# An identity product written ahead of TensorE's waits in the second block of a two-block transformer kernel

## The chip, the cores and the metric

The kernel runs on one core of a Trainium2 chip. A core has TensorE (PE: matrix products; its weight loads are listed apart as PEld), VectorE (DVE), ScalarE (ACT), GpSimd (POOL) and SyncE (SP, which here only starts DMAs). Each engine runs its own instruction stream in order, and the streams meet at semaphores. The metric is the device time of one execution in microseconds (us), the median of several runs.

## The reference, cut to what matters

The input is one sequence of 512 tokens of width 1024, with 256 tokens of context and 256 of memory; all is float32. The first block (adaLN modulation, an RWKV, a neighbourhood attention and a convolution side by side, then a mixture of 16384 tiny experts whose rows are gathered by index) ends in `rmsnorm(xl, final_g)`. The second block, in which the change lies, then has two layers:

```
for layer in range(DEPTH_2):
    x = x + mixers[layer](rms_norm(x, mix_norms[layer]))
    xn, mn, wq, wkv, wo = xattn[layer]
    x = x + memory_cross_attention(rms_norm(x, xn), rms_norm(mem, mn), wq, wkv, wo)
    fn, wg, wu, wd = ffns[layer]
    x = x + swiglu(rms_norm(x, fn), wg, wu, wd)
return rms_norm(x, final_norm)
```

`mixers[0]` is a sliding-window attention beside a multi-head latent attention, `mixers[1]` a mixture of dilated windows; both have rotary positions. Attention is causal, so the second half of the tokens needs the keys of the first, but not the other way round.

## The kernel before

All of it is written by hand: for each engine there is one Python function a stage (`..._pe`, `..._act`, `..._dve`), which issues that engine's instructions in the order in which they are to run, with waits on semaphores. `wait_ge(signal, key)` waits until another engine has done a step; `claim(("bank", b), ...)` waits until a PSUM bank (there are eight) has been read by its last user. Activations lie transposed, the 1024 features over 8 chunks of 128 partitions, and tokens in the free dimension.

The second block is done in two halves of 256 tokens, h=0 and h=1. **Half 0** (1947 to 3156 us of the trace) is woven into the first block's expert stage: `peer_steps` hands the streams of both to each engine, and the second block's share advances in step with a cost that each function yields (`yield 4 * MM`, MM = 427 ns; PE, ACT and DVE must yield the same costs). Meanwhile POOL gathers the rows of the experts for tokens 256 to 511 and DVE multiplies and adds them; in that stretch PE has no expert work. **Half 1** (3156 us to the end) has the core to itself.

The stages of a half, on PE, are those of `second_pe`:

- `experts_pe`: 16 transposes that bring the experts' sums into the transposed layout.
- `scale_pe`, eight times a half: the RMS norm ahead of a stage. PE multiplies the squares by a matrix of ones (L2726, four products of 256 columns), ACT takes the root, DVE the reciprocal and then scales the eight chunks (L2751), and only then can the next products (L2681, in `product_pe`) start. Before it, PE waits until the last residual has been added (DVE), squared (ACT, L2700) and summed.
- `inputs_pe`, `latent_pe`, `dilated_pe`, `cross_pe`: the projections. `rotate_pe` (L3072) multiplies by a rotation matrix for the rotary positions, after ACT has copied the projection out of PSUM (L3065).
- `units_pe`: the attention, in units of one head and 128 queries. `unit_order` sets a pipeline: scores of unit u+1 (L2943), perhaps a store of a finished pair (transpose L2963, copied by ACT L3001 or DVE L3058), a piece of the next projection as filling (`fill.take`), the transposes of unit u's weights (L2950) after ACT's exponential, and the output of unit u-1 (L2957, 64 columns a product; 128 in the cross attention). The latent and dilated projections are the filling of the even and the dilated units; it runs out some units before the end, and the cross attention (8 units, twice a half) has none.
- `out_pe` and `ffn_pe`: long rows of products (L2681, L3447) that wait only for weights from HBM.

PSUM bank 0 holds sums of the first block and is not used by the second; `k.ident` is the 128x128 identity in SBUF.

Of the kernel before, what the change touches and what calls it, by code (L numbers as in the profile page):

```python
# [15 lines left out]
P = 128  # L16
# [2451 lines left out]
MM = 427  # L2468
# [183 lines left out]
    return x.rearrange("p (a b) -> p a b", b=TH)  # L2652


def load_wide(k, p, key, pieces, over=None):

    d = p.next_wide()
    for u in (2 * d, 2 * d + 1):
        p.claim(("w", u), k.S.proj_filled, over or key)
    for j, (dst, src) in enumerate(pieces(k.wide[d])):  # L2660
        p.e.dma_start(dst, src).then_inc(*p.up(k.S.landed(f"wide{d}"), (key, j)))
# [56 lines left out]
def scale_pe(k, p, a, tag, source):  # L2718

    S = k.S  # L2720
    p.wait_ge(S.residual_summed, (source, 2))
    p.wait_ge(S.residual_squared, (source, 3))
    p.claim(("bank", 3), S.norm_root, tag)
    parts = (a.sum[:, 0:TH], a.sum[:, TH:T], a.sq[:, 0:TH], a.sq[:, TH:T])
    for j, x in enumerate(parts):
        ins = p.e.matmul(k.bank[3][:, 0:TH], k.ones, x, start=j == 0, stop=j == 3, skip_group_check=True)  # L2726
    ins.then_inc(*p.up(S.norm_filled, tag))
    yield 4 * MM
    yield 2000
    yield 2000  # L2730
# [71 lines left out]
def experts_pe(k, p, a, tag):  # L2802
    S, e, h = k.S, k.peer, a.h_id
    for t in (2 * h, 2 * h + 1):
        for added in tile_combined(k, t):
            p.wait_ge(*added)
    for i in range(4):
        p.claim(("bank", 4 + i), S.residual_added, (tag, i))
        for c in (2 * i, 2 * i + 1):
            for t in range(2):  # L2810
                ins = p.e.transpose(k.bank[4 + i][:, c % 2 * TH + t * P:c % 2 * TH + t * P + P],
                                    e.ACC[2 * h + t][:, c * P:c * P + P], k.ident)
        ins.then_inc(*p.up(S.proj_filled, (tag, i)))
        yield 800


# [103 lines left out]


def units_pe(k, p, a, name, units, fill, rate):
    S = k.S
    for step, u in unit_order(units):
        x, key = units[u], (name, u)
        if step == "fill":
            yield from fill.take(rate, min(u + 1, len(units) - 1))
        elif step == "rest":
            yield from fill.rest()
        elif step == "pause":  # L2930
            yield unit_cost(x)
        elif step == "scores":
            yield from fill.until(x.mark, u - 1)
            for ready in x.ready:
                p.wait_ge(*ready)
            b = 2 + u % 2
            if x.nb < x.m:
                p.claim(("bank", b), S.weights_exp, key)
            else:
                p.claim(("bank", b), S.scores_low if x.sink is None else S.scores_biased, key)  # L2940
            c0 = 0
            for j, keys in enumerate(x.keys):
                ins = p.e.matmul(k.bank[b][:, c0:c0 + keys.shape[1]], x.q, keys, start=True, stop=True, skip_group_check=True)  # L2943
                c0 += keys.shape[1]
            ins.then_inc(*p.up(S.scores_filled, key))
        elif step == "weights":
            p.wait_ge(S.weights_exp, key)
            p.claim(("bank", 4), (S.act_weights, S.dve_weights)[u % 2], key)
            for j in range(x.m // P):
                ins = p.e.transpose(k.bank[4][:, j * P:j * P + P], a.S[u % 2][:, j * P:j * P + P], k.ident)  # L2950
            ins.then_inc(*p.up(S.weights_filled, key))
        elif step == "output":
            p.wait_ge((S.act_weights, S.dve_weights)[u % 2], key)
            p.wait_ge(*x.values_at)
            p.claim(("bank", 5), S.output_scaled, key)
            for j, values in enumerate(x.values):
                ins = p.e.matmul(k.bank[5][:, 0:x.w], a.PT[u % 2][:, j * P:j * P + P], values, start=j == 0,  # L2957
                                 stop=j == len(x.values) - 1, skip_group_check=True)
            ins.then_inc(*p.up(S.output_filled, key))
        elif step == "store":  # L2960
            p.wait_ge(S.output_scaled, key)
            p.claim(("bank", 4), (S.act_stored, S.dve_stored)[x.tile % 2], key)
            p.e.transpose(k.bank[4][:, 0:P], a.O[x.tile], k.ident).then_inc(*p.up(S.store_filled, key))  # L2963
# [104 lines left out]

def rotate_pe(k, p, a, j, out, rot, key, rows=P):
    n = out.shape[1]  # L3070
    p.wait_ge(k.S.raw_ready, key)
    p.e.matmul(out, rot[0:rows, 0:rows], a.raw[0:rows, j, 0:n], start=True, stop=True, skip_group_check=True).then_inc(  # L3072
        *p.up(k.S.rotation_filled, key))
# [146 lines left out]
def latent_pe(k, p, a):  # L3220

    S, h = k.S, a.h_id
    n = TH * (h + 1)
# [10 lines left out]
    uq = [landed_wide(k, p, ("uq", h, j))[:, 0:1152].rearrange("p (c n) -> p c n", n=384) for j in range(2)]  # L3234
    ukv = landed_wide(k, p, ("ukv", h)).rearrange("p (c n) -> p c n", n=D)
    heads = ukv.rearrange("p c (h n) -> p c h n", n=P)
    p.wait_ge(S.normed, (("latent", h), 4))
    for t in range(2 * h + 2):
        p.claim(("bank", 6), S.act_emptied, ("latent_v", h, t))
# [622 lines left out]
```

## Time and profile before

| | us |
|---|---|
| median of 3 runs | 4306.85 |
| the three runs | 4305.0 to 4326.61 |
| profiled execution | 4309.87 |
| its span, first to last instruction | 4308.0 |

The page of the profile gives PE 3514.9 us busy (82% of the span), PEld 2569.9 (60%), DVE 2216.5 (51%), POOL 1369.1 (32%) and ACT 710.7 (16%). The mean clock that was granted to TensorE is 0.875 of full speed; it has two levels, 1.2 and 2.4 GHz (0.50 and 1.00 in the views). A row of the timeline is a merged run of like instructions: start, length, engine, line, operation, tiles, shape, count, and in brackets how long the engine sat idle before it and what ended that. An ordinary float32 product of the kernel is two MATMUL records in the trace, a transpose is one.

### The profile page before, as it was taken

How to read it: one execution, taken by the hardware profiler on the slowest of the kernel's cores; microseconds unless marked ns; L12 is line 12 of the kernel's file. 1: busy time of each engine (PE TensorE's matmuls, PEld its weight loads, DVE VectorE, ACT ScalarE, POOL GpSimd, SP SyncE). 2: the span in 40 equal slices, each digit the busy share in tenths (PEclk: the TensorE clock that was granted, in tenths of full speed). 3: DMA queues.
4: the chain of work that ended last, by engine and by line, in shares of the span. 5: the costliest groups of instructions: out<-in, count | busy, mean ns of one | idle time of the engine just before them, and what ended most of it. 6: DMA issues, size and time to landing. Idle time of an engine off the chain costs nothing. (4 is left out here: it accounts for less than half of the span.)

```text
span 4308.0 us, 39665 instructions
## 1 busy us (share of the span) xinstructions
PE 3514.9 (82%) x14550; PEld 2569.9 (60%) x14550; DVE 2216.5 (51%) x4375; ACT 710.7 (16%) x1582; POOL 1369.1 (32%) x1215
## 2 busy tenths in 40 slices
PE   7888987887667777756778988779877889999898
PEld 3446657786323343424456776667754678777687
DVE  2443144445887878867677568776543310132201
ACT  2112122221211111111211001210012110021100
POOL 0550012211566666764245555455400000000000
PEclk9887898998888898987688999889977889997999
DMA  6320300004899899997479999889920134321343
GB/s 194 88 86 10 91 25 1 1 22 139 301 328 339 320 356 329 379 336 290 142 254 333 387 368 320 278 281 391 348 81 30 49 104 151 129 86 40 98 150 105
DMA packets 452343, 835.61 MB, mean 194 GB/s; under 512 B 46707, under 2 KB 294574, under 8 KB 452142
## 3 DMA queue, kind: packets, MB, share of 16 engines
q0 software_dynamic: 147456, 536.94, 34.0%
q1 hardware_dynamic: 304694, 296.13, 21.7%
q8 instruction: 117, 1.92, 0.2%
q14 instruction: 76, 0.62, 0.0%
HBM read 830.80 MB, written 2.17 MB: 193 GB/s over the span
## 5 line engine op out<-in xcount | busy, mean ns | idle before, releaser
L2681 PE MATMUL banks<-arena 128*128 128x256 f32 (+1 forms) x4992 | 1167.5, 394 | 92.7 <-DVE arena L2751 44.6
L2681 PEld LDWEIGHTS banks<-arena 128*128 128x128 f32 (+1 forms) x4992 | 983.1, 199 | 270.5 <-issue 67.1
L2246 POOL DMA_INDIRECT arena<-in_peer_u,arena x512 | 571.8, 1117 | 577.2 <-DVE arena L2375 221.7
L2246 POOL DMA_INDIRECT arena<-in_peer_v,arena x512 | 576.6, 1126 | 445.3 <-DVE arena L2361 282.7
L2375 DVE CUSTOM_DVE_ANT_0 arena<-arena 128x1024 f32<-128x1024 f32 x512 | 628.1, 1227 | 101.0 <-DMA arena<-in_peer_u,arena 84.4
L2319 PE MATMUL banks<-arena 128*128 128x512 f32 x768 | 416.5, 686 | 237.7 <-ACT arena L2337 157.6
L2319 PEld LDWEIGHTS banks<-arena 128*128 128x128 f32 x768 | 156.2, 217 | 463.6 <-issue 262.1
L2361 DVE SCALAR_TENSOR_TENSOR arena<-arena 128x1024 f32<-128x1024 f32 x316 | 406.2, 1286 | 29.6 <-DMA arena<-in_peer_v,arena 19.4
L3447 PE MATMUL banks<-arena 128*128 128x256 f32 x1408 | 310.5, 378 | 0.0
L3489 DVE TENSOR_TENSOR arena<-banks,arena 128x512 f32<-128x512 f32 x44 | 30.5, 692 | 538.2 <-PE banks L2681 538.2
L3447 PEld LDWEIGHTS banks<-arena 128*128 128x128 f32 x1408 | 266.2, 189 | 37.8
L835 PE MATMUL banks<-arena 128*128 128x512 f32 (+1 forms) x320 | 136.1, 574 | 28.4 <-ACT arena L962 11.6
L2943 PE MATMUL banks<-arena 64*128 64x256 f32 (+6 forms) x384 | 145.6, 490 | 3.8 <-issue 2.6
L3468 ACT ACTIVATE arena<-banks 128x512 f32<-128x512 f32 x44 | 26.3, 598 | 703.8 <-PE banks L2681 703.7
L548 PE MATMUL banks<-arena 128*128 128x512 f32 (+1 forms) x384 | 140.9, 527 | 0.0
L2950 PE MATMUL banks<-arena 128*128 128x128 f32 x360 | 87.9, 345 | 64.6 <-ACT arena L3001 35.2
L2957 PE MATMUL banks<-arena 128*128 128x64 f32 (+1 forms) x720 | 136.3, 333 | 2.2 <-DVE arena L3052 2.2
L2957 PEld LDWEIGHTS banks<-arena 128*128 128x128 f32 x720 | 132.5, 262 | 6.0 <-issue 5.0
L2986 ACT ACTIVATE arena<-arena 128x256 f32<-128x256 f32 (+3 forms) x128 | 69.4, 542 | 388.8 <-DVE arena L3025 287.9
L2950 PEld LDWEIGHTS banks<-arena 128*128 128x128 f32 x360 | 52.5, 172 | 119.4 <-issue 61.0
L2063 PE MATMUL banks<-arena 128*128 128x512 f32 (+1 forms) x320 | 118.6, 522 | 3.5 <-ACT arena L1841 3.5
L510 POOL TENSOR_TENSOR arena<-arena 128x2048 f32<-128x2048 f32 x16 | 57.3, 3601 | 198.0 <-ACTq L278 105.7
(328 smaller groups left out, 4108.6 us busy)
## 6 DMA issues: line engine op xcount, KB each, us to landing
arena<-in_l_w_gate SPq DMA_DIRECT2D x44, 1024.0 KB, 6.8
arena<-in_l_w_up SPq DMA_DIRECT2D x44, 1024.0 KB, 9.2
arena<-in_l_w_down SPq DMA_DIRECT2D x44, 1024.0 KB, 5.6
arena<-in_ada_w SPq DMA_DIRECT2D x24, 1024.0 KB, 8.1
arena<-in_l_w_qkv SPq DMA_DIRECT2D x24, 1024.0 KB, 8.4
arena<-in_w_in SPq DMA_DIRECT2D x36, 512.0 KB, 4.0
arena<-in_l_w_out SPq DMA_DIRECT2D x16, 1024.0 KB, 5.2
arena<-in_peer_q_w SPq DMA_DIRECT2D x20, 512.0 KB, 7.0
```

The costliest lines, as they stand in the source:

```text
L548: ins = p.e.matmul(k.bank[b][0:m, 0:n], k.W[slot][:, c, 0:m], rhs(c), start=c == 0, stop=c == c_n - 1, skip_group_check=True)
L835: ins = p.e.matmul(k.bank[b][0:m, 0:n], k.W[slot][:, c, 0:m], rhs(c), start=c == 0, stop=c == c_n - 1, skip_group_check=True)
L2063: ins = p.e.matmul(k.bank[4][:, cols], ws[j][:, c, :], k.HT[:, c, cols], start=c == 0, stop=c == DC - 1, skip_group_check=True)
L2246: p.e.indirect_dma_start(e.ring[slot], None, tables[table], bass.IndirectOffsetOnAxis(ap=e.IDX[h][:, t, j:j + 1], axis=0)).then_inc(*p.up( ...
L2319: ins = p.e.matmul(k.bank[b], e.diag[x % 4], e.ring[slot][:, half * T:half * T + T], start=h == 0 and j == 0, stop=h == HEADS - 1 and j == ...
L2361: p.e.scalar_tensor_tensor(out=e.ACC[t], in0=e.ring[slot], scalar=factor, in1=e.ACC[t], op0=ALU.mult, op1=ALU.add).then_inc(*p.up(S.rows_a ...
L2375: p.e.tensor_tensor_reduce(out=e.prod, in0=e.ring[slot], in1=e.H2[:, t, :], scale=1.0, scalar=0.0, op0=ALU.mult, op1=ALU.add, accum_out=e. ...
L2681: ins = p.e.matmul(out, left(c), right(c), start=c == 0, stop=c == c_n - 1, skip_group_check=True)
L2943: ins = p.e.matmul(k.bank[b][:, c0:c0 + keys.shape[1]], x.q, keys, start=True, stop=True, skip_group_check=True)
L2950: ins = p.e.transpose(k.bank[4][:, j * P:j * P + P], a.S[u % 2][:, j * P:j * P + P], k.ident)
L2957: ins = p.e.matmul(k.bank[5][:, 0:x.w], a.PT[u % 2][:, j * P:j * P + P], values, start=j == 0, stop=j == len(x.values) - 1, skip_group_che ...
L3447: ins = p.e.matmul(k.bank[4 + o // 2][:, o % 2 * TH:o % 2 * TH + TH], w[:, r, P * o:P * o + P], a.hid[:, (i - 1) % 2, TH * r:TH * r + TH], ...
```

## The change

A new function `occupied(k, p, n)` issues n products of the identity with itself into the first 128 columns of bank 0. Nothing reads that bank afterwards, and no wait, signal or yielded cost is added. It is called

- 8 times over (n=8) ahead of the first wait of `scale_pe`, and 8 more right behind its four products, that is, ahead of the wait for the scaled chunks;
- with n=2 behind each of the four groups of transposes in `experts_pe`, with n=2 ahead of the wait in `rotate_pe`, and with n=8 ahead of the wait of `latent_pe` for its normed inputs;
- with n=1 in `units_pe` ahead of the waits of `weights` and of `output`, in units whose filling came to less than 4 * MM.

```diff
+def occupied(k, p, n):
+
+    for _ in range(n):
+        p.e.matmul(k.bank[0][:, 0:P], k.ident, k.ident, start=True, stop=True, skip_group_check=True)
...
 def scale_pe(k, p, a, tag, source):
 
     S = k.S
+    occupied(k, p, 8)
     p.wait_ge(S.residual_summed, (source, 2))
     p.wait_ge(S.residual_squared, (source, 3))
     p.claim(("bank", 3), S.norm_root, tag)
...
     ins.then_inc(*p.up(S.norm_filled, tag))
+    occupied(k, p, 8)
     yield 4 * MM
...
         ins.then_inc(*p.up(S.proj_filled, (tag, i)))
+        occupied(k, p, 2)
         yield 800
...
         if step == "fill":
-            yield from fill.take(rate, min(u + 1, len(units) - 1))
+            filled = 0
+            for n in fill.take(rate, min(u + 1, len(units) - 1)):
+                filled += n
+                yield n
...
         elif step == "weights":
+            if filled < 4 * MM:
+                occupied(k, p, 1)
             p.wait_ge(S.weights_exp, key)
...
         elif step == "output":
+            if filled < 4 * MM:
+                occupied(k, p, 1)
             p.wait_ge((S.act_weights, S.dve_weights)[u % 2], key)
...
 def rotate_pe(k, p, a, j, out, rot, key, rows=P):
     n = out.shape[1]
+    occupied(k, p, 2)
     p.wait_ge(k.S.raw_ready, key)
...
     heads = ukv.rearrange("p c (h n) -> p c h n", n=P)
+    occupied(k, p, 8)
     p.wait_ge(S.normed, (("latent", h), 4))
```

It comes to 544 identity products, 282 in half 0 and 262 in half 1. In half 1 they are 8 in `experts_pe`, 128 in `scale_pe`, 32 in `rotate_pe`, 8 in `latent_pe` and 86 in `units_pe` (31 in the even units, 23 in the dilated ones, 32 in the two cross attentions). In half 0 the even units have 51. On the other engines nothing changes.

On PE, the dilated units of half 1 where the filling ends. The rows of before: transposes (L2950), outputs (L2957), scores (L2943), a store (L2963):

```order
L2681 MATMUL banks<-arena 128x256 x8
L2950 MATMUL banks<-arena 128x128 x3
L2957 MATMUL banks<-arena 128x64 x4
L2943 MATMUL banks<-arena 128x256 x2
L2963 MATMUL banks<-arena 128x128
L2950 MATMUL banks<-arena 128x128 x3
L2957 MATMUL banks<-arena 128x64 x3
L2943 MATMUL banks<-arena 128x256 x2
L2950 MATMUL banks<-arena 128x128 x4
```

The same place in the changed kernel, where L2964, L2973, L2955 and L2979 are those four lines and L2658 is the identity product:

```order
L2687 MATMUL banks<-arena 128x256 x8
L2964 MATMUL banks<-arena 128x128 x3
L2973 MATMUL banks<-arena 128x64 x4
L2955 MATMUL banks<-arena 128x256 x2
L2979 MATMUL banks<-arena 128x128
L2658 MATMUL banks<-arena 128x128
L2964 MATMUL banks<-arena 128x128 x3
L2658 MATMUL banks<-arena 128x128
L2973 MATMUL banks<-arena 128x64 x3
L2955 MATMUL banks<-arena 128x256 x2
L2658 MATMUL banks<-arena 128x128
L2964 MATMUL banks<-arena 128x128 x4
```

From the first unit without filling on, one product stands ahead of the transposes and one ahead of the outputs of each unit.

On PE, the end of that stage: the output projection, the norm ahead of the second cross attention, and that attention's first unit, before:

```order
L2963 MATMUL banks<-arena 128x128
L2681 MATMUL banks<-arena 128x256 x64
L2726 MATMUL banks<-arena 128x256 x4
L2681 MATMUL banks<-arena 128x256 x32
L2943 MATMUL banks<-arena 128x256 x2
L2950 MATMUL banks<-arena 128x128 x2
```

and now:

```order
L2979 MATMUL banks<-arena 128x128
L2687 MATMUL banks<-arena 128x256 x64
L2658 MATMUL banks<-arena 128x128 x8
L2733 MATMUL banks<-arena 128x256 x4
L2658 MATMUL banks<-arena 128x128 x8
L2687 MATMUL banks<-arena 128x256 x32
L2955 MATMUL banks<-arena 128x256 x2
L2658 MATMUL banks<-arena 128x128
L2964 MATMUL banks<-arena 128x128 x2
```

Eight products fill the wait on each side of the norm's four.

## Rows read from the trace of the kernel before

**Rows 1.** The page: clock granted to TensorE in 40 slices, tenths of full speed.

```profile
PEclk9887898998888898987688999889977889997999
```

**Rows 2.** Busy time of each engine, granted clock and DMA by stretch.

```profile
core 0: us, PE busy (x) PEld busy (x) DVE busy (x) ACT busy (x) POOL busy (x), PEclk, DMA share, GB/s
...
2047.00:2191.00 144.00, 101.25 (x320) 65.69 (x320) 91.25 (x247) 31.55 (x107) 33.88 (x37) 0.62 0.50 153
...
2344.00:2563.00 219.00, 196.65 (x859) 168.38 (x860) 141.19 (x173) 13.92 (x19) 123.69 (x108) 0.95 1.03 389
...
2730.00:2763.00 33.00, 24.13 (x79) 16.87 (x79) 21.87 (x65) 7.79 (x29) 8.43 (x9) 0.50 0.58 181
...
3244.00:3317.00 73.00, 50.30 (x178) 31.60 (x177) 28.64 (x99) 20.11 (x59) 0.00 (x0) 0.81 0.05 15
3317.00:3406.00 89.00, 75.86 (x282) 48.00 (x282) 31.57 (x104) 22.20 (x59) 0.00 (x0) 0.69 0.07 24
...
3907.50:3960.00 52.50, 45.98 (x164) 37.29 (x164) 15.42 (x51) 10.97 (x29) 0.00 (x0) 0.50 0.03 10
...
4017.00:4036.00 19.00, 11.79 (x67) 7.88 (x67) 8.75 (x29) 6.21 (x23) 0.00 (x0) 1.00 0.02 7
```

**Rows 3.** Timeline of PE, dense projection rows at full clock, half 1.

```profile
3212.47 3.73 PE L3127 MATMUL banks<-arena 128*128 128x128 f32 x32
```

**Rows 4.** Timeline of PE, first cross attention of half 1.

```profile
3459.26 0.44 PE L2950 MATMUL banks<-arena 128*128 128x128 f32 x2 [1.70 <-ACT arena L2990]
...
3464.14 1.06 PE L2957 MATMUL banks<-arena 128*128 128x128 f32 x4
...
3484.79 0.48 PE L2963 MATMUL banks<-arena 128*128 128x128 f32 x1 [0.52 <-DVE arena L3052]
```

**Rows 5.** Timeline of PE, second cross attention of half 1.

```profile
4017.10 0.44 PE L2950 MATMUL banks<-arena 128*128 128x128 f32 x2 [1.70 <-ACT arena L2990]
...
4021.31 0.61 PE L2957 MATMUL banks<-arena 128*128 128x128 f32 x4
...
4036.38 0.33 PE L2963 MATMUL banks<-arena 128*128 128x128 f32 x1 [0.52 <-DVE arena L3052]
```

**Rows 6.** Timeline of PE, end of the dilated units, half 1.

```profile
3904.49 1.00 PE L2957 MATMUL banks<-arena 128*128 128x64 f32 x8
3905.43 1.13 PE L2943 MATMUL banks<-arena 64*128 64x256 f32 x4
...
3907.78 0.77 PE L2950 MATMUL banks<-arena 128*128 128x128 f32 x3 [0.97 <-DVE arena L3058]
...
3917.31 1.09 PE L2950 MATMUL banks<-arena 128*128 128x128 f32 x4 [1.39 <-ACT arena L3001]
3918.19 1.81 PE L2957 MATMUL banks<-arena 128*128 128x64 f32 x8
...
3923.94 2.07 PE L2943 MATMUL banks<-arena 64*128 64x256 f32 x4
...
3927.24 0.87 PE L2950 MATMUL banks<-arena 128*128 128x128 f32 x3 [0.82 <-DVE arena L3058]
...
3960.34 30.65 PE L2681 MATMUL banks<-arena 128*128 128x256 f32 x128
```

**Rows 7.** Chain that ended last within 3900 to 3965 us, by line.

```profile
by line: PE banks L2943 28.1%; PE banks L2957 27.5%; PE banks L2950 16.8%; PE banks L2681 12.8%; DVE arena L3025 5.0%; issue 2.9%; ACT arena L2986 2.2%; PE banks L2963 1.5%; DVE arena L3052 1.4%; DVE arena L3058 1.0%; ACT arena L3001 1.0%; 
```

**Rows 8.** Timeline of PE, norms of half 1 and what follows them.

```profile
3741.77 3.75 PE L2726 MATMUL banks<-arena 128*128 128x256 f32 x8 [4.11 <-ACT arena L2700]
3748.49 10.03 PE L2681 MATMUL banks<-arena 128*128 128x256 f32 x32 [2.96 <-DVE arena L2751]
...
3992.55 1.97 PE L2726 MATMUL banks<-arena 128*128 128x256 f32 x8 [1.56 <-issue]
3997.48 17.05 PE L2681 MATMUL banks<-arena 128*128 128x256 f32 x64 [2.96 <-DVE arena L2751]
...
4036.55 14.02 PE L2681 MATMUL banks<-arena 128*128 128x256 f32 x64
```

**Rows 9.** Timeline of PE, two rotations among the dilated units of half 1.

```profile
3804.07 1.10 PE L3072 MATMUL banks<-arena 128*128 128x512 f32 x2 [2.08 <-ACT arena L3065]
...
3846.86 2.04 PE L3072 MATMUL banks<-arena 128*128 128x512 f32 x2 [2.02 <-ACT arena L3065]
```

More of the change, by code:

```diff
@@ L2922, in units_pe @@
 def units_pe(k, p, a, name, units, fill, rate):
-    S = k.S
+    S, filled = k.S, 0
     for step, u in unit_order(units):
```

## The prediction

> **What bounds the kernel now.** I read the page first, for the clock row: in 11 of the last 22 slices, which are those of the second block, TensorE is granted less than 0.9 of full speed [rows 1]. Then the table of stretches, to see where that is. The long rows of products run at 0.95 and are bound by DMA in half 0 (DMA share 1.03). The attention stretches are the slow-clocked ones: 0.62, 0.50, 0.81, 0.69 and 0.50, while the second cross attention of half 1 stands at 1.00 [rows 2]. Third, the timeline of PE there. In the last 52.5 us of half 1's dilated units PE is busy for 45.98 us at clock 0.50 [rows 2], and the chain view of 3900 to 3965 us runs for over 85% over PE's own lines [rows 7]. So PE is the bound, and at half speed: eight output records that took 1.00 us just before take 1.81, four score records 2.07 instead of 1.13 [rows 6]. Nothing long was waited for when the clock went: the wait in front of the first slow transposes was 0.97 us, the longest later one 1.39 [rows 6]. In that stage products are short, and the clock stays low until the dense products at 3960.
>
> How the clock reacts is also seen in pairs of like places. The two cross attentions of half 1 are the same code: from its first transposes to its last store one takes 3484.79 - 3459.26 = 25.53 us at half speed, the other 4036.38 - 4017.10 = 19.28 us at full [rows 4, 5]. A norm behind a wait of 4.11 us takes 3.75 us for its ones products against 1.97 behind 1.56 us; 64 product records behind a norm take 17.05 us where 64 behind no wait take 14.02 [rows 8]. A rotation behind 2.08 us of waiting ran at full speed (1.10), another behind 2.02 us at half (2.04) [rows 9]. The waits are near a border where it can go either way.
>
> **The price of an added product.** 32 records of 128 columns take 3.73 us at full speed, so 0.117 each at most, and a product is two of them: 0.22 us (two such records at the pace without the last one's tail) [rows 3]. At half speed four such records take 1.06 instead of 0.61 us, so a product costs 0.43 to 0.45 us [rows 4, 5]. 544 of them are 120 us at full speed; what counts is how much does not fit into waits.
>
> **Where they fit.** Ahead of the norms: 8 products are 1.76 us. The wait behind a feed-forward is 4.11 us, behind an output projection 1.56 plus the last product's tail of about 0.16, so they cost 0 to 0.1 us. Behind the ones products: 1.76 us in a wait of 2.96 us [rows 8]; at half speed they are 3.5 us and would overshoot by some 0.4. At rotations 0.44 us lie in about 2.0 [rows 9]. In a unit, the product ahead of the transposes lies in a wait only where a store came before (0.97 and 1.39 us, two units in four [rows 6]); the one ahead of the outputs lies in none, since the copy of those weights was done a unit earlier. That one is on PE's path: 0.22 us a unit, and where there is no store 0.44.
>
> **What comes back if the clock holds, half 1.**
> - End of the dilated units. Four units take 3927.24 - 3907.78 = 19.46 us, of which 2.2 are waits, so 17.2 is PE at half speed [rows 6]; at full speed that is 8.9. The waits for DVE and ACT do not shrink, and with a faster PE they grow: I put 3.1 us in place of 2.2, for 12.0. The added products not covered by waits are 2 x 0.22 + 4 x 0.22 = 1.3. So 13.3 for 19.46; over the stretch of 52 us (2.7 times four units) 16.5 us come back. The 128 records behind it take 30.65 us, at 14.02 for 64 they would take 27.9 [rows 6, 8]: 2.8. Together 19.
> - Cross attentions: the first gains 25.53 - 19.28 = 6.25, and both pay 8 x 0.22 = 1.8: net 2.7.
> - Latent part. 3317 to 3406 us: clock 0.69 is 62% of 89 us at half, 55 us, of which PE is busy 0.85, 47 us; half of it is 23. Against it stand 31 products, two thirds uncovered, 4.5, and waits that grow, 3. Net 16. From 3244 to 3317 the filling is always 4 MM or more, so hardly a product is added and the alternating clock (0.81) stays; 1 us from one rotation.
> - Norms. The one at 3741 gives 1.8 for its own products and 10.03 - 7.0 = 3.0 for those behind it (32 records at 14.02 / 64 each); the one at 3992 gives 17.05 - 14.02 = 3.0 [rows 8]. There are eight of them a half: of the others two lie behind a wait of about 10 us which 1.8 us of products do not fill, and give 1 to 3 behind them; the last one and the transposes behind it give 3. Together 14.
> - Two rotations at half speed give 0.9 each and as much for the products behind: 3.
>
> Sum: 19 + 2.7 + 17 + 14 + 3 = 56 us.
>
> **Half 0.** The same stages: 33 us at 0.50 (end of the dilated units), 144 at 0.62 (latent) [rows 2], two cross attentions. By the same steps: 8, a third of the 38 us that 144 us would yield (109 us at half speed, PE 0.70 busy) = 12 because waits for DVE, which also sums expert rows, are longer and more of the clock falls remain, 3, norms 10, rotations 3, together 36. Not all of it reaches the end: in its product rows DMA is full (1.03), and DVE does expert rows between block steps [rows 2]. Bounds for what passes are nothing and all; I take a little over half, as the attention stretches themselves have DMA free (0.50, 0.58): 20.
>
> Forecast: 56 + 20 = 76 us less. The profiled execution would go from 4309.87 to about 4234, and the median, 3 us below that, from 4306.85 to **4231**.
>
> **Rivals.**
> - *Clock holds, half 0 passes nothing or all.* 4251 or, with all 36, 4215; with waits that do not grow, the latent and dilated terms at 23 and 25 and half 0 full, about 113 less: 4194. Same mechanism, another size.
> - *Only the long waits are mended.* The clock does not fall at norms and rotations (14 + 3 + 1, 10 + 3 in half 0), but units of short products still drop it, as they did behind 0.97 us of wait, and then pay 0.43 us a product. Gains about 25, costs as in the next rival 25: about 4305. The Trainium skill (TensorE: Matmul & The Clock Gate, section on what is actually happening) says that the ramp costs less than 1% of a typical kernel span; by that at most 43 us are to be had in all, 4264. The rows speak against both: half speed in the dilated end alone costs 19 us, and that end is not behind a long wait [rows 6].
> - *The identity product does not count for the clock, or too little (slower).* It is mostly zeros. Then all slow stretches stay slow and each product on PE's path costs 0.43. End of the dilated units: 8 x 0.43 = 3.4 per four units, 0.9 covered, 2.5, times 2.7 is 7; first cross 4 x 0.9 = 3.5, second 1.8; latent 31 x 0.43 x 0.7 = 9; eight norms at half speed 2; half 1: 23, half 0, where waits are longer, 11. 4341. It decides itself at the first unfilled units: if 3907 to 3960 is still at 0.50, this has won. For it speaks only that the trace has no such product; against it that every other kind of product raised the clock.
> - The same page, in its section on PE-mode transpose, says that transposes do not bring the full clock. The change uses a plain matrix product, so by that page it counts; the sum is the same.
>
> **How the numbers follow.** Forecast as worked out 0.60; same mechanism with more or less of it 0.18; only long waits 0.13; slower 0.09. A measurement of this kernel can tell about 0.5% (21.5 us) from no change. Faster by more: 0.60 + 0.18 + a little of the third = 0.80. Within 0.5%: 0.12. Slower: 0.08. The range leaves out the slower rival and the outer part of the third: 4194 to 4295.
>
> **What would show it.** In the profile after: the stretch of the last dilated units of half 1 at clock above 0.9 and about 36 us long; both cross attentions of half 1 near 21 us; ones products of norms behind feed-forwards 1.97 us; the mean clock above 0.93; the added line busy at 0.22 us a product. Wrong, if the clock in the units stays at 0.50, if half 0 (1947 to 3156) does not get shorter though its clock rises, or if the waits for ACT and DVE in the units grow by what PE saves.

## The result, and the profile after

The changed kernel takes 4260.29 us, the median of 4 runs (4257.88 to 4275.26), against 4307.60 for the kernel before beside it (4305.0 to 4326.61): ratio 0.9883, with a 95% interval of 0.9857 to 0.9909. A second measurement with more rounds gave 4257.57 against 4309.04, 0.9882 (0.9857 to 0.9907). The two medians are 47 and 51 us below the kernel before; the forecast was 76, so 4260 lies inside the range and 29 us above the number.

Where the time went is read by stretches. First the table of stretches for half 0 and half 1 as wholes, of the kernel before, then of the kernel after (the columns are those of [rows 2]: start:end, length, busy time of each engine with its instructions in brackets, granted clock, DMA share, GB/s):

```profile
1947.00:3155.50 1208.50, 980.82 (x4059) 791.94 (x4060) 848.69 (x1354) 176.93 (x399) 566.36 (x488) 0.85 0.83 300
3155.50:4308.00 1152.50, 1019.54 (x4451) 828.69 (x4450) 245.74 (x606) 158.97 (x363) 0.00 (x0) 0.89 0.30 95
```

```profile
1942.70:3161.80 1219.10, 1033.62 (x4622) 855.44 (x4623) 848.29 (x1354) 177.03 (x399) 571.56 (x489) 0.89 0.82 297
3161.80:4258.30 1096.50, 1009.50 (x4976) 839.78 (x4974) 245.74 (x606) 159.13 (x363) 0.00 (x0) 0.97 0.31 100
```

**Half 1 is 56.0 us shorter (1152.5 to 1096.5), half 0 is 10.6 us longer.** In half 1 the clock went from 0.89 to 0.97, and PE, with 525 more instructions, was busy for 10 us less and idle for 46 us less (133.0 to 87.0). In half 0 the clock went up as well, from 0.85 to 0.89; PE was idle for 42 us less (227.7 to 185.5), but busy for 53 us more. The other 4 us lie ahead of half 0, where nothing was changed; that part ends between 1940 and 1980 us from kernel to kernel in the traces of this study.

The page's clock row of after, to be set beside [rows 1]: its last 11 slices, half 1, read 8, 8 and then nine times 9; in half 0, the 11 slices ahead of them, values of 7 and 8 remain.

```profile
PEclk9888988999888898979788999799988999999999
```

By stages (each cut runs from one norm's ones products to the next norm's; the last to the end), half 1 of the kernel before: sliding-window and latent attention; first cross attention; feed-forward; dilated attention; second cross attention; feed-forward; last norm.

```profile
3182.10:3437.10 255.00, 214.20 (x842) 152.80 (x843) 78.41 (x235) 53.27 (x142) 0.00 (x0) 0.81 0.15 47
3437.10:3502.20 65.10, 51.47 (x209) 40.00 (x209) 19.99 (x47) 13.56 (x34) 0.00 (x0) 0.79 0.23 73
3502.20:3741.80 239.60, 232.52 (x1065) 202.09 (x1065) 17.41 (x26) 12.14 (x19) 0.00 (x0) 0.99 0.46 149
3741.80:3992.60 250.80, 227.46 (x1017) 184.81 (x1017) 72.46 (x191) 46.03 (x108) 0.00 (x0) 0.85 0.19 62
3992.60:4052.20 59.60, 45.84 (x209) 36.30 (x209) 20.01 (x47) 13.51 (x34) 0.00 (x0) 0.94 0.25 79
...
4291.70:4308.00 16.30, 9.18 (x24) 5.57 (x24) 7.02 (x11) 2.84 (x4) 0.00 (x0) 0.50 0.16 64
```

The same six of after:

```profile
3188.60:3424.90 236.30, 205.73 (x985) 154.46 (x986) 78.33 (x235) 53.43 (x142) 0.00 (x0) 0.92 0.16 51
3424.90:3483.10 58.20, 50.21 (x274) 41.22 (x273) 20.02 (x47) 13.43 (x34) 0.00 (x0) 1.00 0.26 81
3483.10:3721.40 238.30, 234.81 (x1098) 204.10 (x1098) 17.40 (x26) 12.15 (x19) 0.00 (x0) 1.00 0.46 150
3721.40:3947.20 225.80, 211.04 (x1126) 175.09 (x1127) 72.49 (x191) 46.07 (x108) 0.00 (x0) 0.99 0.21 69
3947.20:4005.50 58.30, 50.32 (x274) 41.33 (x274) 20.01 (x47) 13.54 (x34) 0.00 (x0) 1.00 0.26 81
...
4243.80:4258.30 14.50, 8.17 (x40) 6.09 (x40) 7.02 (x11) 2.83 (x4) 0.00 (x0) 0.79 0.18 72
```

Line by line: 18.7, 6.9, 1.3, 25.0, 1.3 and 1.8 us less, with 1.2 for the second feed-forward. The gain sits where the clock was low, and DVE and ACT are busy for as long as before in every stage.

Half 0, from its second norm to its third (sliding-window and latent attention), before and after:

```profile
1974.00:2222.40 248.40, 188.68 (x707) 138.45 (x707) 177.15 (x365) 48.06 (x141) 91.60 (x85) 0.73 0.66 223
```

```profile
1968.50:2227.90 259.40, 206.88 (x889) 161.67 (x890) 177.00 (x365) 48.15 (x141) 92.81 (x85) 0.81 0.64 215
```

This stage alone is 11.0 us longer, about as much as all of half 0: the clock rose from 0.73 to 0.81, the idle time fell by 7 us, and PE was busy for 18 us more. Part of the 11 may be chance: the other two traces with products in half 0 took 256.2 and 253.5 us for it, and the seven with the full experts' work and no products there 248.4 to 255.0.

The end of the dilated units of half 1, timeline of PE after (start, length, operation; in brackets the idle time ahead and who ended it). L2658 is the added product, L2964 the transposes, L2973 the outputs; the rows answer to [rows 6]:

```profile
3894.93 0.52 PE L2964 MATMUL banks<-arena 128*128 128x128 f32 x3 [0.74 <-DVE arena L3074]
...
3901.68 0.63 PE L2964 MATMUL banks<-arena 128*128 128x128 f32 x4 [1.30 <-ACT arena L3017]
3902.15 0.39 PE L2658 MATMUL banks<-arena 128*128 128x128 f32 x2
3902.37 1.00 PE L2973 MATMUL banks<-arena 128*128 128x64 f32 x8
...
3908.31 0.52 PE L2964 MATMUL banks<-arena 128*128 128x128 f32 x3 [0.74 <-DVE arena L3074]
...
3917.74 27.89 PE L2687 MATMUL banks<-arena 128*128 128x256 f32 x128
3945.46 1.95 PE L2658 MATMUL banks<-arena 128*128 128x128 f32 x16
3947.24 1.92 PE L2733 MATMUL banks<-arena 128*128 128x256 f32 x8
```

Four units take 3908.31 - 3894.93 = 13.38 us, where they took 19.46; eight output records are back at 1.00. The waits are about as long as before (0.74 and 1.30 us, with a product already inside them), yet the clock stays up. The added line costs (3947.24 - 3945.46) / 8 = 0.22 us a product.

Now the same place in half 0, the end of its dilated units, before and after:

```profile
2736.93 0.66 PE L2950 MATMUL banks<-arena 128*128 128x128 f32 x2 [1.62 <-ACT arena L3001]
...
2748.59 0.66 PE L2950 MATMUL banks<-arena 128*128 128x128 f32 x2 [1.68 <-ACT arena L3001]
```

```profile
2740.62 0.66 PE L2964 MATMUL banks<-arena 128*128 128x128 f32 x2 [1.37 <-ACT arena L3017]
2741.07 0.64 PE L2658 MATMUL banks<-arena 128*128 128x128 f32 x2
2741.50 0.95 PE L2973 MATMUL banks<-arena 128*128 128x64 f32 x4
...
2754.62 0.66 PE L2964 MATMUL banks<-arena 128*128 128x128 f32 x2 [1.42 <-ACT arena L3017]
```

Two transposes take 0.66 us in both: half speed in both. Four units went from 11.66 to 14.00 us. Here the products are paid for (2741.50 - 2741.07 = 0.43 us each) and buy nothing. The stretch of the table says it too:

```profile
2738.00:2771.00 33.00, 29.03 (x106) 22.74 (x106) 18.55 (x55) 5.85 (x23) 6.57 (x7) 0.50 0.44 127
```

### The profile page after: what moved, and what is told of

Read it like the earlier page. It is cut to its first block and busy times, and to the rows that moved or that the text cites. A ratio compares the mean times of both kernels' runs of the same rounds, so it can differ in the third digit from the quotient of the medians.

```text
span 4258.3 us, 41827 instructions
## 1 busy us (share of the span) xinstructions
PE 3555.5 (83%) x15638; PEld 2641.1 (62%) x15638; DVE 2219.7 (52%) x4375; ACT 711.5 (17%) x1582; POOL 1379.1 (32%) x1215
## 3 DMA queue, kind: packets, MB, share of 16 engines
q8 instruction: 125, 2.05, 0.2%
## 5 line engine op out<-in xcount | busy, mean ns | idle before, releaser
L2687 PE MATMUL banks<-arena 128*128 128x256 f32 (+1 forms) x4992 | 1142.1, 388 | 78.3 <-DMA arena<-in_l_w_up 35.4
L2687 PEld LDWEIGHTS banks<-arena 128*128 128x128 f32 (+1 forms) x4992 | 954.9, 194 | 254.3 <-issue 40.9
L2246 POOL DMA_INDIRECT arena<-in_peer_v,arena x512 | 588.8, 1150 | 446.0 <-DVE arena L2361 284.9
L2319 PEld LDWEIGHTS banks<-arena 128*128 128x128 f32 x768 | 156.6, 217 | 461.0 <-issue 265.7
L3465 PEld LDWEIGHTS banks<-arena 128*128 128x128 f32 x1408 | 265.6, 189 | 38.3
L2658 PE MATMUL banks<-arena 128*128 128x128 f32 x1088 | 189.0, 302 | 0.0
L2658 PEld LDWEIGHTS banks<-arena 128*128 128x128 f32 x1088 | 171.3, 217 | 22.2 <-issue 16.9
L2955 PE MATMUL banks<-arena 64*128 64x256 f32 (+6 forms) x384 | 124.8, 430 | 3.0 <-issue 2.3
L835 PEld LDWEIGHTS banks<-arena 128*128 128x128 f32 x320 | 63.3, 207 | 92.9 <-issue 81.4
L1566 POOL TENSOR_TENSOR arena<-arena 64x256 f32<-64x256 f32 x24 | 19.1, 796 | 313.4 <-ACT arena L1465 312.5
```

The lines of the kernel that those rows point to most:

```text
L835: ins = p.e.matmul(k.bank[b][0:m, 0:n], k.W[slot][:, c, 0:m], rhs(c), start=c == 0, stop=c == c_n - 1, skip_group_check=True)
L2246: p.e.indirect_dma_start(e.ring[slot], None, tables[table], bass.IndirectOffsetOnAxis(ap=e.IDX[h][:, t, j:j + 1], axis=0)).then_inc(*p.up( ...
L2319: ins = p.e.matmul(k.bank[b], e.diag[x % 4], e.ring[slot][:, half * T:half * T + T], start=h == 0 and j == 0, stop=h == HEADS - 1 and j == ...
L2658: p.e.matmul(k.bank[0][:, 0:P], k.ident, k.ident, start=True, stop=True, skip_group_check=True)
L2687: ins = p.e.matmul(out, left(c), right(c), start=c == 0, stop=c == c_n - 1, skip_group_check=True)
L3465: ins = p.e.matmul(k.bank[4 + o // 2][:, o % 2 * TH:o % 2 * TH + TH], w[:, r, P * o:P * o + P], a.hid[:, (i - 1) % 2, TH * r:TH * r + TH], ...
```

## The experiments

Theory A: the products keep TensorE's clock up, half 1 gives the whole gain, and half 0 passes little of it on, because DVE's expert rows set its pace. Rival B: half 0 gets 20 us shorter, as the forecast had it. (The expectations of the first two runs also name a "Theory B", which is another thing: the products of half 0 neither cost nor gain.) Rival C: what counts is any instruction in PE's stream that keeps it issuing, not the load. Each kernel ran beside the kernel before on the same chip; the ratio is to that one. The first four share one chip, the next three another, the last four a third; the kernel before took 4321.9, 4318.52 and 4307.51 us there.

**One half alone.** Of the 544 products, 262 are in half 1 and 282 in half 0.

```diff
-def occupied(k, p, n):
+def occupied(k, p, a, where, n):
-    for _ in range(n):
+    for _ in range(n if a.h_id == 1 else 0):
```

> The change in half 1 only (262 products). Theory A: the gain is made in half 1 alone, where TensorE is on the path, and the products of half 0 cost 6 to 11 us: about 4308 - 56 = 4252, and half 1 takes 1096 us. Theory B: the products of half 0 neither cost nor gain, the 11 us there are chance of where the clock falls: 4260. If half 0 gave something hidden: above 4265.

Measured: 4285.23 us (4275.8 to 4295.31) against 4321.9, ratio 0.9911 (0.9877 to 0.9945). Its four times form two pairs, 4275.8 and 4277.18, 4293.28 and 4295.31. In the median that is 37 us less, not 56: by its own expectation the result lies on the side of "half 0 gave something hidden", although the faster pair is 45 us less and the intervals of this kernel and of the change overlap. The profiled one is of the upper pair, its half 1 took 1122.2 us, and its timeline shows what the 17 us are:

```profile
3898.87 0.33 PE L2979 MATMUL banks<-arena 128*128 128x128 f32 x1
3899.04 0.39 PE L2658 MATMUL banks<-arena 128*128 128x128 f32 x2
3900.73 0.78 PE L2964 MATMUL banks<-arena 128*128 128x128 f32 x4 [1.31 <-ACT arena L3017]
3901.31 0.63 PE L2658 MATMUL banks<-arena 128*128 128x128 f32 x2
...
3911.74 0.88 PE L2964 MATMUL banks<-arena 128*128 128x128 f32 x3 [0.39 <-DVE arena L3074]
...
3934.07 0.88 PE L2964 MATMUL banks<-arena 128*128 128x128 f32 x3 [0.39 <-DVE arena L3074]
```

At 3899 a product takes 0.39 us in the display, behind the wait of 1.31 it takes 0.63: the clock fell there, although the same instructions with the same 1.30 us of wait held it in the profile of the change. From then on four units take 3934.07 - 3911.74 = 22.3 us, 2.9 more than without the products. So the products make the fall less likely; they do not exclude it: the dilated stage took 250.8, 250.8, 250.8, 250.8 and 246.8 us in the five traces without products in its units, and 224.8 to 225.8 us in five of the eight traces that have them, or the transposes in their place, at full size, 249.5 (this one), 244.9 and 243.3 in the other three. Where the clock falls, the same code costs instead of saving, until the next dense row.

The opposite half:

```diff
-    for _ in range(n):
+    for _ in range(n if a.h_id == 0 else 0):
```

> The change in half 0 only (282 products). Theory A: 4308 + 6 to 11 = 4314 to 4319, since the clock that comes back there meets waits for DVE, ACT and DMA, and the products in units at half speed lie on the path. Theory B: 4308, within noise. My prediction had it at 4288.

Measured: 4328.19 (4313.1 to 4347.5) against 4321.9, ratio 1.0009 (0.9985 to 1.0033): from 6 us less to 14 us more. Rival B's 20 us less are outside; the 6 to 11 us more of Theory A and the nothing of "Theory B" both lie inside. Its table of stretches for half 0:

```profile
1961.50:3181.80 1220.30, 1032.65 (x4623) 855.32 (x4624) 848.51 (x1354) 176.60 (x399) 564.24 (x489) 0.90 0.82 297
```

Clock 0.90 instead of 0.85, length 1220.3. Half 0 measures 1205.6 to 1217.1 us in the seven traces where it has no products (before, the single-half and other half-1 kernels), and 1214.0, 1219.1 and 1220.3 in the three where it has them: no gain, and a loss of some 7 us of which part may be chance. (On the chip of this run the three without took 1211.1 to 1217.1.)

**Is it the load or the instruction?** Two kernels with products in half 1 only. In one, each is replaced by two transposes of the identity, instruction for instruction at the same places; in the other the same product reads 32 of the 128 rows.

```diff
-        p.e.matmul(k.bank[0][:, 0:P], k.ident, k.ident, start=True, stop=True, skip_group_check=True)
+        for _ in range(2):
+            p.e.transpose(k.bank[0][:, 0:P], k.ident, k.ident)
```

> Half 1 only, and each product is replaced by two transposes of the identity (one trace record each, as a product has two, so the same time). By what the Trainium skill states (TensorE: Matmul & The Clock Gate, PE-mode transpose) transposes do not bring the full clock: 4320 to 4335. If they count as products do, as the 16 transposes ahead of 3157 us in the trace of before suggest, where the clock went up behind them: 4252.

Measured: 4284.49 (4276.06 to 4289.59) against 4321.9, ratio 0.9919 (0.9892 to 0.9946). Half 1:

```profile
3180.00:4274.20 1094.20, 1005.80 (x4975) 831.98 (x4973) 245.71 (x606) 159.00 (x363) 0.00 (x0) 0.98 0.32 101
```

Transposes do what the products do: clock 0.98, half 1 in 1094.2 us, and the ratio is that of the run half1 (0.9911). The Trainium skill (TensorE: Matmul & The Clock Gate, section on PE-mode transpose) says that transposes do not bring the full clock. For the transpose instruction as this kernel issues it, float32 against the identity, this trace differs, and the measurement decides.

```diff
-        p.e.matmul(k.bank[0][:, 0:P], k.ident, k.ident, start=True, stop=True, skip_group_check=True)
+        p.e.matmul(k.bank[0][:, 0:P], k.ident[0:32, :], k.ident[0:32, 0:P], start=True, stop=True, skip_group_check=True)
```

> Half 1 only, and each product contracts over 32 partitions of the identity in place of 128: the same 128 columns and the same time on TensorE, a quarter of the array's rows. If the gain is the granted clock, and the clock follows how much of the array works: the clock stays as before and the products cost their time, 4320 to 4335. If any product counts alike: 4252, as with full rows. If the gain were not the clock but something in the order or spacing of the instructions: 4252 too.

Measured: 4390.08 (4386 to 4416) against 4321.9, ratio 1.0157 (1.0131 to 1.0184). Half 1 by the table, and the end of its dilated units:

```profile
3196.70:4414.40 1217.70, 1152.20 (x4976) 917.79 (x4974) 245.92 (x606) 159.94 (x364) 0.00 (x0) 0.87 0.28 90
```

```profile
3998.84 0.79 PE L2658 MATMUL banks<-arena 32*128 32x128 f32 x2
3999.57 1.97 PE L2973 MATMUL banks<-arena 128*128 128x64 f32 x8
```

As many columns in as many instructions, PE busy for 95% of half 1 (92% in the change), and yet the clock of half 1 is 0.87, below the 0.89 without them: rival C falls, since an instruction that keeps PE issuing is not enough, and so does the thought that the order of the instructions makes the gain. The cost was underestimated (4320 to 4335 expected): at half speed such a product takes 3999.57 - 3998.84 = 0.73 us, where a full one takes 0.43. The weight loads in the traces show part of why. The load of a full product begins 0.21 us ahead of the product (3901.10 against 3901.31 in the run half1); that of the small one begins with it at 3998.84, and PEld sat idle for 0.33 us before. Eight small ones in a row are hardly dearer (2.05 us at full speed, 1.95 for full ones). So this kernel differs from the change in two things, in the load and in these gaps, and no run here tells which of them keeps the clock down.

**Which products.** Half 1 only, those of the attention units alone (86), then those of the norms alone (128).

```diff
-    for _ in range(n if a.h_id == 1 else 0):
+    for _ in range(n if a.h_id == 1 and where == "unit" else 0):
```

> Half 1, and only the 86 products in the attention units (none at norms, rotations, the latent start). My prediction's terms (dilated end 19, cross 2.7, latent 16): up to 38 us less, 15 to 20 less in those executions in which the clock falls at the entry of the dilated end. If the long waits at norms and rotations are what counts, and the units only pay: 0 to 10 us more.

Measured: 4286.95 (4275.58 to 4303.01) against 4318.52, ratio 0.9915 (0.9892 to 0.9939). As good as all 262 within the intervals. Its times spread over 27 us, and in the profiled one the dilated stage took 243.3 us, not 225.8: this execution lost the clock there. Its first stage is 16 us shorter than before (255.1 to 238.7), as much as the forecast's latent term.

The second kernel has `where == "norm"` in that line.

> Half 1, and only the 128 products at the eight norms. My prediction's term: 14 us less, seen at the norms behind feed-forwards (3.75 to 1.97 us for the ones products) and in the 32 to 64 products behind each norm; the units stay as before. If the clock behind a norm carries over into the units: the first cross attention at full speed as well, 20 less. If 8 products overshoot the short waits: 5 less or nothing.

Measured: 4314.56 (4308.27 to 4349.16) against 4318.52, ratio 0.9998 (0.9971 to 1.0026). In its trace half 1 is 3.6 us shorter than before (1148.9). The two feed-forwards and the dilated stage gain 6.5 us, and the second cross attention's stage loses 5.4, because there the clock fell in this execution:

```profile
3991.10:4056.10 65.00, 54.77 (x242) 43.85 (x241) 19.99 (x47) 13.48 (x34) 0.00 (x0) 0.79 0.23 72
```

The norms' products alone are worth nothing that can be measured. That what they mend is given back in the next attention is how this one trace has it; whether the other executions lost it in the same place is not known.

**Only where PE waits.** Products in half 1 only; none ahead of outputs; ahead of transposes only behind a store, there 4 (cross) or 6 (other units) where ACT copies the store, and 2 or 4 where DVE does; seven ahead of each latent value after the first, 32 in place of 8 at the latent start; 28 in place of 8 ahead of the half's first norm and the last. The lines that differ from the change, less those of the norms and the latent start:

```diff
-            if filled < 4 * MM:
-                occupied(k, p, 1)
+            if filled < 4 * MM and stored is not None:
+                occupied(k, p, a, "unit", (4 if x.w == P else 6) if stored % 2 == 0 else (2 if x.w == P else 4))
+            stored = None
             p.wait_ge(S.weights_exp, key)
...
-            if filled < 4 * MM:
-                occupied(k, p, 1)
...
+        if t:
+            occupied(k, p, a, "latent", 7)
         p.claim(("bank", 6), S.act_emptied, ("latent_v", h, t))
```

> Half 1 only, with the products put where PE waits: in the units none ahead of outputs and none where no store came before, but 6 or 4 ahead of the transposes behind a store (4 or 2 in the cross attention); 7 ahead of each latent value product that waits for ACT, 32 for the latent start, 28 ahead of the two norms behind waits of 10 us. If the products ahead of outputs lie on the path, 0.22 us each, and the alternating clock of 3244 to 3317 costs some 7 us: 15 to 20 us less than the same half with the products as in the change (half 1 about 1080 us), and no dilated end at half speed. If the products ahead of outputs cost nothing because the waits behind them shrink as much: within 8 us of it.

Measured: 4255.35 (4250.2 to 4263.28) against 4318.52, ratio 0.985 (0.9806 to 0.9894), half 1 in 1086.0 us, 10.5 less than in the change. The end of the dilated units:

```profile
3875.53 0.52 PE L2965 MATMUL banks<-arena 128*128 128x128 f32 x3
...
3886.35 1.06 PE L2658 MATMUL banks<-arena 128*128 128x128 f32 x8
3887.48 0.52 PE L2965 MATMUL banks<-arena 128*128 128x128 f32 x3
```

Four products in a row, with no wait left behind them, and four units in 3887.48 - 3875.53 = 11.95 us instead of 13.38. The second cross attention takes 19.29 us from its first transposes to its last store, as it did before the change at full clock (19.28, [rows 5]), where the change takes 20.37. So the products outside waits cost what they were priced at, and the clock is held without them. The expectation of 15 to 20 us was too high all the same, since the dilated stage as a whole gained only 1.0 us. Of the 10.5 us, 5.6 are in the first stage (latent), 1.9 at the first norm, the rest in the cross and dilated stages and at the last norm; the parts were not tried one by one. This is the fastest version, though its interval and that of the change overlap, and the two did not run on one chip.

**What sets the pace of half 0.** Two pairs, each with and without the change. In the first pair the expert rows of tokens 256 to 511 are gathered at half their width, from other places of the tables, while DVE works on 1024 columns as before; in the second DVE too works on 512. Neither computes the experts' sums for these tokens as it should. The first pair says what DMA holds back. The second lightens DMA and DVE together, so it says what DVE holds back once DMA is light; DVE's work alone was not halved in any run.

```diff
-        p.e.indirect_dma_start(e.ring[slot], None, tables[table], bass.IndirectOffsetOnAxis(
+        place, rows = e.ring[slot], tables[table]
+        if t >= 2:
+            place, rows = place[:, 0:T], rows.rearrange("n (a b) -> (n a) b", b=T)
+        p.e.indirect_dma_start(place, None, rows, bass.IndirectOffsetOnAxis(
...
```

> The kernel before, with the gathered expert rows of tokens 256 to 511 half as wide (2 KB in place of 4, from other places of the tables), DVE's work on them unchanged; that part of the result is wrong by it. It is the base for the next one. If half 0 is bound by DMA in its feed-forwards and not elsewhere: half 0 gets shorter by the waits for weights, 45 us, and not by more.

> The same with the change in both halves. If DMA takes back what the clock gives in half 0: against the last one 56 us less in half 1 and 20 to 36 less in half 0. If it is DVE's expert rows between block steps, or the clock itself does not hold there: 56 less in all, half 0 within 10 us of equal.

Measured: 4249.23 without and 4210.6 with the change (ratios 0.9852 and 0.977 to the kernel before): 39 us for the change. Half 0 of the two traces:

```profile
1955.90:3097.10 1141.20, 957.59 (x4058) 779.51 (x4059) 848.56 (x1354) 177.16 (x399) 548.80 (x491) 0.87 0.63 205
```

```profile
1951.60:3095.80 1144.20, 1010.37 (x4622) 844.62 (x4623) 848.34 (x1354) 176.79 (x399) 546.52 (x490) 0.91 0.63 204
```

Half 0 without the change got 67 us shorter by the narrow rows (1208.5 to 1141.2; 45 were expected), so DMA does hold it back. But with DMA share down from 0.83 to 0.63 the change still gives nothing in half 0, so DMA is not what takes the change's gain. Half 1 gave 37.6 us in this pair and not 56 (1153.0 to 1115.4), because the profiled execution lost the clock in the dilated stage (244.9 us).

```diff
...
+                x = slice(0, T if t >= 2 else D)
-                p.e.tensor_tensor_reduce(out=e.prod, in0=e.ring[slot], in1=e.H2[:, t, :], scale=1.0, scalar=0.0, op0=ALU.mult,
+                p.e.tensor_tensor_reduce(out=e.prod[:, x], in0=e.ring[slot][:, x], in1=e.H2[:, t, x], scale=1.0, scalar=0.0, op0=ALU.mult,
...
```

> As narrow_before, and DVE's multiply and add over those rows half as wide too (1024 to 512 columns); half of that part of the expert sums is left out. Base for the next. Waits of PE for DVE's block work in half 0 should shrink by 0.6 us each, some 50 to 100 us in all.

> The same with the change. If DVE's expert rows are what half 0 waits for: 56 less in half 1 and 20 to 36 less in half 0 against light_before. If the clock in half 0 does not hold because there are too few products for its longer waits, then with shorter waits it holds: the same gain. If neither: half 0 equal, 56 less in all.

Measured: 4197.16 without and 4132.45 with the change (0.9743 and 0.9601): 65 us. Half 0 of the two traces:

```profile
1946.80:3050.10 1103.30, 955.39 (x4059) 777.63 (x4060) 586.12 (x1354) 177.14 (x399) 521.37 (x491) 0.87 0.65 211
```

```profile
1939.70:3025.10 1085.40, 979.79 (x4623) 821.83 (x4624) 585.63 (x1354) 177.25 (x399) 520.19 (x491) 0.94 0.66 215
```

With DVE busy for 586 us instead of 849, the change makes half 0 17.9 us shorter, and its clock reaches 0.94. What differs between the pairs is PE's busy time. The idle time falls by 42 us in the original pair, by 50 in the narrow and by 42 in the light one; the busy time grows by 53, 53 and 24. Had DVE's full rows taken back what a faster PE saves, the idle time would have fallen by less in the first two pairs than in the light one, and it did not; PE's waits for DVE fell in the original pair too (80.7 to 70.7 us in all). The light rows let more of the clock come back: both pairs stand at 0.87 without the change, and at 0.91 and 0.94 with it. That is the second branch of the expectation above, in which shorter waits let the clock hold. It rests on one trace each, and the light one with the change is the fastest of its kernel's four times (4122.58, median 4132.45). Yet the end of its dilated units stays slow even here:

```profile
2655.00:2676.00 21.00, 19.50 (x71) 15.26 (x70) 9.78 (x36) 4.17 (x15) 4.72 (x5) 0.50 0.22 64
```

and the whole dilated stage takes 209.8 us with the products and 209.9 without. The gain is in the first stage (237.5 to 232.7 us, clock 0.75 to 0.87) and in the first cross attention (69.1 to 62.9 us, clock 0.78 to 1.00; in the original pair it stayed at 0.79, and 71.8 became 73.5).

## Why the prediction was right or wrong, point by point

**What bounds the kernel, and that the products hold the clock: right.** The slower rival had put its test at the first unfilled units of half 1. They ran at 1.00, not 0.50; the identity's zeros did not keep it from counting. The rival of long waits alone falls with the same rows. The prediction took a bound of 43 us for it from the Trainium skill (TensorE: Matmul & The Clock Gate, section on what is actually happening: the ramp costs under 1% of a typical kernel span). That bound was misread: the section gives the figure for the ramp at the start of a kernel, and here the clock fell and rose all through the second block. Half 1 alone gave back 56 us, 1.3% of the span and 5% of its own length. No run here measures the ramp at the start.

**Half 1: right in its sum and in most terms.** Forecast 56, measured 56.0. That it agrees to the last digit is luck: two other traces with the same products give 1095.8 and 1095.6 us for half 1, two more 1115.4 and 1122.2, which is 30 to 57 us less than the 1152.5 of before.
- The dilated end: four units forecast at 13.3, measured 13.38; the stretch of 52.56 us [rows 6: 3907.78 to 3960.34] took 36.2 (forecast 36); the 128 records behind it 27.89 (forecast 27.9).
- Cross attentions: forecast near 21 each, both 20.37. The cost of the eight units' products was put at 1.8 and is 20.37 - 19.28 = 1.1, since those ahead of transposes fit into waits more often than assumed.
- Latent: forecast 17 with one rotation; its stage, which also holds the products behind a norm, is 18.7 shorter.
- Norms: forecast 14. The rows that were looked at agree (ones products 3.75 to 1.97 behind the feed-forward at 3721, 1.8 at the last norm). As a whole the term was not measured: latent, norms and rotations together gave 56 - 19.2 (dilated end) - 4.1 (cross attentions) = 32.7, forecast 34. Taken alone the norms' products gave 3.6 us in the trace and no measurable time (norms1), so most of the term needs the units' products beside it. The terms of this sum are not independent, which the working did not say.
- Products outside waits: priced at 1.3 us per four units. The kernel with none there is 13.38 - 11.95 = 1.43 faster: right.
- Two sums of the rivals do not come out of their own terms: the "about 113" behind the range's lower end adds up to some 105 (4202, not 4194), and "costs as in the next rival 25" stands beside 23 + 11 = 34 there. Neither touches the forecast.

**Half 0: wrong, and this is the whole miss.** The failed step is "By the same steps: 8, a third of the 38 us ... = 12 ..., together 36", of which 20 were to pass. Measured: 10.6 us more in the profiles of the change, 1.0009 (0.9985 to 1.0033) for half 0 alone. The prediction blamed what might not reach the end; what failed comes before that, the 36 us themselves. PE was to be busy for less, and was busy for 53 us more, while its idle time fell by 42.
- *The dilated end (8).* The step carried half 1's reaction over to units that are not the same. In half 0 a unit has fewer records (1 or 2 transposes for 3 or 4, 2 or 4 outputs for 6 or 8) beside waits for ACT that are not shorter (1.62 and 1.68 us, 1.39 in half 1). One product ahead of each wait did not raise the clock (0.50 in the change, 0.50 with light experts), and four units took 14.00 - 11.66 = 2.3 us more. The wait rows for this were in the trace and were not set against half 1's.
- *Latent, cross attentions, norms, rotations (28).* Here the clock did rise, but too little: in the first stage from 0.73 to 0.81 (half 1's went from 0.81 to 0.92), in the first cross attention not at all in the profile of the change (0.79; 0.88 in that of half0). At a low clock an added product costs 0.43 us and not 0.22, and the products outside waits cost more than the clock gave back: the first stage took 248.4 to 259.4 us.
- *What passes (20 of 36).* The fraction was taken from the free DMA of those stretches. DMA did not take the gain (narrow pair: 3 us more). With DVE's expert rows halved as well the change gains 18 us in half 0, and the rows show it as a higher clock, not as waits that stop growing. "DVE does expert rows between block steps" was in the text, and what it does to the clock was not priced. That DVE's rows act through the length of PE's waits fits these rows and was not tested by itself.

The prediction named its own refutation, half 0 not shorter though its clock rises; that is what happened. Its mark of a mean clock above 0.93 was missed as well, at 0.91, since half 0 stayed at 0.89.

**The steadiness of the gain** was not considered. Whether a stretch keeps its clock differs between executions of the same kernel when it is near the border (half1: 17 us between its pairs of times). All ten timed runs of the change lie between 4250.8 and 4275.3, so this hit it little; the profiled execution of narrow_after lost 19 us in its dilated stage by it.

**Left open.** How much of the loss in half 0, some 7 us and 10.6 in the profiles, is the price of products outside waits and how much is chance. Also why half 1 with products alone gained 37 us in the median (45 in its faster pair) where the full change gained 47 to 51: half 0's products may make the state in which half 1 begins better, or the chips differ; nothing here tells these apart. So Theory A holds in that half 0 passes nothing on and that the gain is made in half 1; that half 1's products alone give all of it is not shown.

## What to carry to other kernels

Where TensorE runs at half clock in a stretch of short products between short waits, work that nobody reads, put into the waits themselves, can bring the clock back at next to no cost (half 1 was 66 us shorter in the kernel whose attention units had products only there); put outside a wait, it costs its full time, and twice that where the clock does not come back. So before carrying a gain from one stage to a similar one, compare the size of the work between the waits and the length of the waits, not the code, and look afterwards at PE's busy and idle time apart: a higher clock with more busy time is no gain.

## What the runs showed of the hardware

- The clock fell after waits of 0.97 us [rows 6] and 1.31 us (half1) amid short products, and it held through 1.30 us with the same instructions (the change). The length of the wait alone does not decide it.
- Transposes of the identity hold the clock as well as products (0.98 in half 1).
- Products of 32 rows, with the gaps that they bring, do not hold it (0.87). Single ones cost 0.73 us at half speed where one of 128 rows costs 0.43; eight in a row cost 2.05 us at full speed against 1.95.
